# Finer pieces for the expert stages: mid-pass token turns, bf16 routing entries and a three-product down projection

## The chip, the cores and the metric

The kernel runs on one core of a Trainium2 chip. The metric is the device time of one execution in microseconds; less is better.

## The reference, cut to what matters

A two-layer backbone over 256 latent tokens and 256 context tokens of width 1024. Each layer has a token mixer (windowed attention in layer 0, a gated recurrence in layer 1) and then a mixture of experts. Layer 0's mixture runs on 512 tokens, layer 1's on 256.

```python
scores = sigmoid(t @ router_w)                      # 64 experts, 8 groups, top 8 of 4 groups
w = take(scores, idx) / sum * 2.5                   # gain of each (token, expert)
y = (silu(x @ w_gate[e]) * (x @ w_up[e])) @ w_down[e] * w   # x: the tokens routed to e
out = sum over the 8 experts of a token + shared expert
```

Each expert has three float32 matrices: gate and up of 1024 x 256, down of 256 x 1024, so 3 MiB in all.

## The kernel before

**Routing (`route_phase`).** For every token and expert the kernel writes an entry of three float32 numbers (`routes.entry`: token index less 8192, gain, destination row less 8192) and a slot number (`routes.slot`). The work is cut into blocks of S slots of one expert, S = 128 in layer 0 and 64 in layer 1. The phase also starts loading the first blocks' weights (`weights.prefetch`), once the normed rows are stored, and adds the shared expert's output.

**First expert stage (`expert_phase`, layer 0).** One block b after the other, 66 in this run. Two buffers q = b % 2 hold gate/up weights and down weights. Step b runs on five engines at once, each with its instruction order written out by hand and semaphores between them:

- TensorE (`step`, `down`, `turn_tokens`, `slots`): the gate and up products of block b in 4 chunks of 2 k-slices. Each float32 product is three float32r products (`x_hi*w_hi`, `x_lo*w_hi`, `x_hi*w_lo`), 24 matmuls of 512 columns (L1340). Then the 8 transposes of block b+1's tokens (L1313), the down projection of block b-1 in plain float32 (L1325; 4 matmuls, shown as 8 records), 2 transposes of block b's hidden rows (L1351), and the entry selection of block b+3 with a one-hot matrix (L1301; 4 matmuls, 8 records).
- ScalarE rounds block b+1's weights to float32r (`w_hi`, L1383, 4 chunks), writes `x_hi` (L1373), the SiLU (L1400), half of y (L1390) and the transposed hidden rows (L1407).
- VectorE subtracts to get `w_lo` (L1459, 4 chunks) and `x_lo` (L1451), multiplies the hidden rows with the gain (L1478), copies half of y (L1467), builds the one-hot matrix of block b+4 (`pick`, L1433, one instruction per token tile) and reads entries from PSUM (`indices`, L1442 and L1443). Its order in a step: w_lo chunks 0, 1, 2; hidden; w_lo chunk 3; x_lo; y; pick; indices.
- GpSimd only issues indirect DMAs: the scatter of block b-1's y rows (L1266) and the gather of block b+3's tokens (L1257).
- SP issues the weight loads (L899, L902), 1 MiB each. A gate/up load waits until the buffer's `w_lo` is made, a down load until the down projection that read the buffer is done (`y_done`).

**Second expert stage (`expert_pair_phase`, layer 1).** Two blocks of 64 slots side by side make a pair, 33 pairs in this run. All products are plain float32 (L1630, L1657). There is one buffer for gate, one for up and one for down; each is loaded again when the products that read it are done. SP's order: gates, ups, downs of pair i.

The code of the routing phase's entries and of both stages as they are before:

## Time and profile before

| | |
|---|---|
| median of 3 runs | 2326.23 us (2323.54 to 2328.62) |
| the profiled execution's own time | 2326.45 us |
| its span, first to last instruction | 2324.6 us |
| mean granted TensorE clock | 0.915 of full speed |
| TensorE busy | 1915.4 us (82%) |
| VectorE busy | 1145.3 us (49%) |
| ScalarE busy | 794.1 us (34%) |
| GpSimd busy | 318.6 us (14%) |
| HBM read and written | 596 MB and 56 MB |

PE is TensorE, PEld its weight loads, DVE VectorE, ACT ScalarE, POOL GpSimd; SP only issues DMAs. The end of a matmul is modelled and matmuls overlap, so for TensorE the distance from one start to the next is the time that counts. In a row of the timeline the first number is the start in us, the second the duration of the merged instructions, xN their count, and the bracket tells how long the engine idled before and what released it.

### The profile page before, as it was taken

What the parts mean: (1) busy time and instruction counts of PE and PEld (TensorE: products, weight loads), DVE (VectorE), ACT (ScalarE), POOL (GpSimd) and SP (SyncE); (2) the same over time, 40 slices, a digit from 0 to 9 for tenths busy, and PEclk for the clock granted to TensorE, in tenths of its full rate; (3) what the DMA queues carried; (4) which work ended last, traced back from release to release, by engine and by line L of the source; (5) the groups of instructions that cost most, each with busy time, mean ns of one, the idle gap of its engine ahead of it and who ended that gap; (6) DMA issues with size and microseconds to landing.
All of it is one profiled execution on the core that took longest, in us unless ns stands there. A gap on an engine that the chain in (4) does not pass through costs nothing. (4 is left out here: it accounts for less than half of the span.)

```text
span 2324.6 us, 33561 instructions
## 1 busy us (share of the span) xinstructions
PE 1915.4 (82%) x9971; PEld 1298.1 (56%) x9972; DVE 1145.3 (49%) x2242; ACT 794.1 (34%) x1292; POOL 318.6 (14%) x333
## 2 busy tenths in 40 slices
PE   2889897899999999999974987637778788878783
PEld 0778744467777777777741971103445555555551
DVE  2325622577777777777748565893131121212114
ACT  1214411155555555555521557870101111111110
POOL 0220010111111211211210101221001111111110
PEclk8999987899999999999987997768889999999997
DMA  6850055068998899999955416304439999999994
GB/s 239 296 188 1 1 224 202 9 251 323 339 339 330 327 342 345 348 333 343 330 191 220 137 55 194 109 18 128 185 144 418 414 392 388 400 411 402 418 366 173
DMA packets 139045, 597.07 MB, mean 257 GB/s; under 512 B 32632, under 2 KB 51128, under 8 KB 79728
## 3 DMA queue, kind: packets, MB, share of 16 engines
q1 hardware_dynamic: 103264, 509.97, 58.3%
q0 software_dynamic: 35584, 84.31, 9.7%
q10 hardware_dynamic: 144, 2.10, 0.2%
q8 instruction: 31, 0.51, 0.1%
q14 instruction: 22, 0.18, 0.0%
HBM read 596.17 MB, written 56.20 MB: 281 GB/s over the span
## 5 line engine op out<-in xcount | busy, mean ns | idle before, releaser
L1459 DVE TENSOR_TENSOR m_w_lo<-m_wgu,m_w_hi 128x1024 fp32r<-128x1024 f32 x264 | 312.6, 1221 | 170.6 <-ACT m_w_hi L1383 157.1
L1383 ACT ACTIVATE m_w_hi<-m_wgu 128x1024 fp32r<-128x1024 f32 x264 | 266.9, 1051 | 205.6 <-DMA m_wgu<-in_moe_w_up 153.0
L1630 PE MATMUL ps<-m_wgu,m_xT 128*64 128x256 f32 x2112 | 261.4, 403 | 78.9 <-DMA m_wgu<-in_moe_w_up 60.1
L1630 PEld LDWEIGHTS ps<-m_wgu,m_xT 128*64 128x64 f32 x2112 | 185.7, 145 | 165.8 <-issue 122.5
L1325 PE MATMUL ps<-m_wd,m_hidT 128*128 128x512 f32 x528 | 237.6, 593 | 0.3 <-ACT m_hidT L1407 0.3
L1340 PE MATMUL ps<-m_w_hi,m_x_hi 128*128 128x512 f32 x528 | 212.8, 403 | 7.2 <-DVE m_x_lo L1451 6.5
L1340 PE MATMUL ps<-m_w_lo,m_x_hi 128*128 128x512 f32 x528 | 208.1, 394 | 0.0
L1340 PE MATMUL ps<-m_w_hi,m_x_lo 128*128 128x512 f32 x528 | 207.2, 392 | 0.0
L1725 DVE SCALAR_TENSOR_TENSOR m_hid<-m_act_g,m_meta,ps 128x256 f32<-128x256 f32 x33 | 15.9, 480 | 337.9 <-ACT m_act_g L1679 337.9
L1325 PEld LDWEIGHTS ps<-m_wd,m_hidT 128*128 128x128 f32 x528 | 95.3, 190 | 95.1 <-issue 95.1
L1266 POOL DMA_INDIRECT y_rows<-h,m_sidx x66 | 67.5, 1023 | 554.5 <-DVE h L1467 554.5
L1657 PE MATMUL ps<-m_wd,m_hidT 128*64 128x512 f32 x528 | 122.3, 604 | 21.2 <-ACT m_hidT L1682 15.3
L1679 ACT ACTIVATE m_act_g<-ps 128x256 f32<-128x256 f32 x33 | 12.6, 383 | 315.7 <-PE ps L1630 315.7
L1340 PEld LDWEIGHTS ps<-m_w_hi,m_x_hi 128*128 128x128 f32 x528 | 100.2, 190 | 27.0 <-issue 7.5
L325 ACT ACTIVATE squares<-x_stream 128x1024 bf16<-128x1024 f32 x16 | 16.9, 1053 | 286.8 <-DVE x_stream L864 143.4
L1340 PEld LDWEIGHTS ps<-m_w_lo,m_x_hi 128*128 128x128 f32 x528 | 99.8, 189 | 21.4
L1340 PEld LDWEIGHTS ps<-m_w_hi,m_x_lo 128*128 128x128 f32 x528 | 100.3, 190 | 19.1
L1798 PE MATMUL ps<-c_rows,table 128*128 128x512 f32 x96 | 52.5, 709 | 51.0 <-DMA c_rows<-y_rows 51.0
L1575 POOL DMA_INDIRECT h<-h_rows,m_gidx x35 | 35.5, 1014 | 379.3 <-DVE m_gidx L1713 373.0
L1451 DVE TENSOR_TENSOR m_x_lo<-ps,m_x_hi 128x512 fp32r<-128x512 f32 x134 | 85.9, 682 | 0.5 <-ACT m_x_hi L1373 0.5
L1657 PEld LDWEIGHTS ps<-m_wd,m_hidT 128*64 128x64 f32 x528 | 42.1, 138 | 78.5 <-issue 78.5
L1433 DVE TENSOR_SCALAR m_onehot<-table,l_slot 128x128 f32<-128x128 f32 x280 | 78.2, 345 | 10.0 <-PE ps L1301 4.8
(316 smaller groups left out, 3429.9 us busy)
## 6 DMA issues: line engine op xcount, KB each, us to landing
m_wgu<-in_moe_w_gate SPq DMA_DIRECT2D x132, 1024.0 KB
m_wgu<-in_moe_w_up SPq DMA_DIRECT2D x132, 1024.0 KB
m_wd<-in_moe_w_down SPq DMA_DIRECT2D x132, 1024.0 KB, 9.9
c_rows<-y_rows SPq DMA_DIRECT2D x12, 2048.0 KB, 15.9
mods<-in_ada_w POOLq DMA_DIRECT2D x11, 1024.0 KB, 6.3
mods<-in_ada_w SPq DMA_DIRECT2D x11, 1024.0 KB, 4.8
mods<-in_lru_w_in SPq DMA_DIRECT2D x7, 1280.0 KB, 6.9
ada_w<-in_ada_w SPq DMA_DIRECT2D x8, 1024.0 KB, 17.5
```

Of the source, the lines that this page charges most:

```text
L325: act.activation(g.junk[:], g.x[:, t, :], ACT.Square, accum_out=g.sumsq[:, t:t + 1]).then_inc(self.squared, 1)
L1266: pool.indirect_dma_start(g.y_rows[0:tiles * P * TOPK, :], bass.IndirectOffsetOnAxis(ap=sidx[q][:, 0:1], axis=0), ysb[q], None, bounds_che ...
L1325: last = pe.matmul(g.ps[0:S, YB + n, :], hidT[:, j, :], wd[:, q, j, n * 512:(n + 1) * 512], start=(j == 0), stop=(j == KF - 1))
L1340: last = pe.matmul(g.ps[0:S, GU, :].rearrange("p (a f) -> p a f", a=2), x[:, q, k, :], w[:, :, k, :], start=(k == 0 and n == 0), stop=(k = ...
L1383: act.activation(w_hi[:, :, k, :], wgu[:, q, :, k, :], ACT.Copy).then_inc(hi_s, 1)
L1433: last = dve.tensor_scalar(onehot[:, q, t, :], g.field("iota")[:, 0:S], routes.slot[:, t, bass.ds(e, 1)], g.table[:, bass.ds(b + FIELD[f"n ...
L1451: dve.tensor_tensor(x_lo[:, q, ks, :], g.ps[:, XB + n, 0:4 * S].rearrange("p (k c) -> p k c", c=S), x_hi[:, q, ks, :].bitcast(F32), ALU.su ...
L1459: dve.tensor_tensor(w_lo[:, :, k, :], wgu[:, q, :, k, :], w_hi[:, :, k, :].bitcast(F32), ALU.subtract).then_inc(lo_s, 1)
L1575: pool.indirect_dma_start(xg, None, g.h2_rows[0:tiles * P, :], bass.IndirectOffsetOnAxis(ap=gidx[:, 0:1], axis=0), bounds_check=last_token ...
L1630: last = pe.matmul(g.ps[half[s], GU, a * FE:(a + 1) * FE], xT[:, k, half[s]], wgu[:, s, a, k, :], start=(k == 0), stop=(k == KD - 1))
L1657: last = pe.matmul(g.ps[half[s], YB + n, :], hidT[:, j, half[s]], wd[:, s, j, n * 512:(n + 1) * 512], start=(j == 0), stop=(j == KF - 1))
L1798: last = pe.matmul(g.ps[:, t % 2, :], g.ident, rows[:, 2 * (t % 2), k, :], start=(k == 0), stop=(k == TOPK - 1))
```

## The change

Five edits, in the order of the kernel:

1. Routing entries become bfloat16. Token index and destination are written as two or three exact pieces, the gain as three bfloat16 pieces found one after the other, so an entry has 9 numbers instead of 3. The constant pieces are written before the router's scores are awaited. The one-hot matrix is bfloat16 too and comes from a single `scalar_tensor_tensor` over all token tiles instead of a `tensor_scalar` for each. `indices` adds the three pieces with a `tensor_reduce` and then makes the index from its result.
2. First stage: the transposes of block b+1's tokens are moved from behind chunk 3 to behind chunk 1 (`TURN_AT = 1`), on ScalarE and VectorE as well.
3. First stage: the down projection becomes three float32r products (12 matmuls of 512 columns instead of 4 float32 ones). ScalarE makes `wd_hi` (2 copies of 128x1024 per block) and `hidT_hi`, GpSimd makes `wd_lo` (2 `tensor_tensor` of 128x1024 per block, `down_low`, ahead of the scatter and the gather in its order), VectorE makes `hidT_lo`. A down load now waits for `wd_lo` instead of `y_done`.
4. First stage: the down buffers and one gate/up buffer are placed in memory of `g.mods` that is free by then. This makes room and moves no data.
5. Second stage: gate and up weights have two buffers instead of one; the prefetch loads pair 1's gate and up as well, and the loops take two pairs a turn. In SP's order `gate_up(n, q)` loads the gates and ups of pair n+1 once the same products of pair n-1 are done.

```diff
-        self.entry = sb(n + "entry", [P, tiles, EXPERTS, 3])
+        self.entry = sb(n + "entry", [P, tiles, EXPERTS, 3 * PIECES], BF16)
...
-        self.wgu = sb(tag + "wgu", [P, 2, 2, KD, FE])
+        self.wgu = sb(tag + "wgu", [P, 2, 2, 2, KD, FE])
...
     def prefetch(self, sp):
...
+        for q in range(2):
+            for s in range(2):
+                self.gate(sp, 2 * q + s, q, s)
+            for s in range(2):
+                self.up(sp, 2 * q + s, q, s)
+            if q == 0:
+                for s in range(2):
+                    self.down(sp, s, s)
...
+                for t in range(tiles):
+                    chain.done(dve.memset(routes.entry[:, t, :, 0], t * P - FAR))
+                    chain.done(dve.memset(routes.entry[:, t, :, DEST * PIECES], TOPK * t * P - FAR))
+                chain.done(dve.memset(routes.entry[:, :, :, 2], 0.0))
+                chain.done(dve.tensor_copy(routes.entry[:, :, :, 1], tok0))
+                chain.done(dve.tensor_scalar(routes.entry[:, :, :, DEST * PIECES + 1], tok0, float(TOPK), None, ALU.mult))
                 dve.wait_ge(scored, 1)
...
-                chain.done(dve.tensor_tensor(routes.entry[:, :, :, 1], weight[:], wsum[:, :, None].to_broadcast([P, tiles, E]), ALU.mult))
-
+                chain.link(dve.tensor_tensor(weight[:], weight[:], wsum[:, :, None].to_broadcast([P, tiles, E]), ALU.mult))
+                for m in range(PIECES):
+                    piece = routes.entry[:, :, :, GAIN * PIECES + m]
+                    chain.link(dve.tensor_copy(piece, weight[:]))
+                    if m + 1 < PIECES:
+                        chain.link(dve.tensor_tensor(weight[:], weight[:], piece, ALU.subtract))
...
-                for t in range(tiles):
-                    chain.link(dve.tensor_scalar(wsum[:, t:t + 1], tok[:, t:t + 1], float(TOPK), -1.0 - FAR, ALU.mult, ALU.add))
-                    chain.done(dve.tensor_scalar(routes.entry[:, t, :, 2], kth[:, t, :], wsum[:, t:t + 1], None, ALU.add))
+                chain.done(dve.tensor_scalar(routes.entry[:, :, :, DEST * PIECES + 2], kth[:], -1.0, None, ALU.add))
...
-                    sp.wait_ge(y_done, b - 1)
+                    sp.wait_ge(wd_lo_s, KF * b - KF)
...
+                def down_low(i, q):
+                    b = 2 * i + q
+                    for j in range(KF):
+                        pool.wait_ge(wd_hi_s, KF * b + (j + 1))
+                        pool.tensor_tensor(wd_lo[:, q, j, :], wd[:, q, j, :], wd_hi[:, q, j, :].bitcast(F32), ALU.subtract).then_inc(wd_lo_s, 1)
+
...
                 with pool.Fori(1, final + 1) as i:
+                    down_low(i, 0)
                     scatter(i - 1, 1)
                     gather(i + 1, 1)
+                    down_low(i, 1)
                     scatter(i, 0)
                     gather(i + 2, 0)
...
-                    pe.wait_ge(hidT_s, b + 1)
-                    pe.wait_ge(wd_in[q], 16 * (i + 1))
+                    pe.wait_ge(hidT_split, b + 1)
+                    pe.wait_ge(wd_lo_s, KF * b + KF)
...
-                        for n in range(2):
-                            last = pe.matmul(g.ps[0:S, YB + n, :], hidT[:, j, :], wd[:, q, j, n * 512:(n + 1) * 512],
-                                             start=(j == 0), stop=(j == KF - 1))
+                        for m, (h, w) in enumerate(((hidT_hi, wd_hi), (hidT_hi, wd_lo), (hidT_lo, wd_hi))):
+                            for n in range(2):
+                                last = pe.matmul(g.ps[0:S, YB + n, :], h[:, j, :], w[:, q, j, n * 512:(n + 1) * 512],
+                                                 start=(j == 0 and m == 0), stop=(j == KF - 1 and m == 2))
...
-                    turn_tokens(i + q, 1 - q)
+                        if c == TURN_AT:
+                            turn_tokens(i + q, 1 - q)
...
                     if split:
-                        split_high(i + q, 1 - q, range(CHUNKS - 1))
+                        split_high(i + q, 1 - q, range(TURN_AT + 1))
+                    tokens(i + q, 1 - q)
+                    if split:
+                        split_high(i + q, 1 - q, range(TURN_AT + 1, CHUNKS - 1))
...
-                    tokens(i + q, 1 - q)
+                    down_high(i, q, range(1))
...
-                    act.activation(hidT[:], g.ps[:, HB, 0:KF * S].rearrange("p (j c) -> p j c", c=S), ACT.Copy).then_inc(hidT_s, 1)
+                    act.activation(hidT_hi[:], g.ps[:, HB, 0:KF * S].rearrange("p (j c) -> p j c", c=S), ACT.Copy).then_inc(hidT_s, 1)
+                    down_high(i, q, range(1, KF))
...
-                    for t in range(tiles):
-                        last = dve.tensor_scalar(onehot[:, q, t, :], g.field("iota")[:, 0:S], routes.slot[:, t, bass.ds(e, 1)],
-                                                 g.table[:, bass.ds(b + FIELD[f"negbase{layer}"][0], 1)], ALU.subtract, ALU.is_equal)
-                    last.then_inc(onehot_s, 1)
+                    dve.scalar_tensor_tensor(onehot[:, q, :, :], routes.slot[:, :, bass.ds(e, 1)].to_broadcast([P, tiles, S]),
+                                             g.table[:, bass.ds(b + FIELD[f"negbase{layer}"][0], 1)],
+                                             g.field("iota")[:, None, 0:S].to_broadcast([P, tiles, S]),
+                                             ALU.add, ALU.is_equal).then_inc(onehot_s, 1)
...
-                    dve.tensor_copy(meta[:, bass.ds(b, 1), :].rearrange("p o c -> p (o c)"), g.ps[0:S, MB + q, 0:3]).then_inc(meta_v, 1)
-                    dve.tensor_scalar(gidx[q][:], g.ps[0:S, MB + q, 0:1], FAR, None, ALU.add).then_inc(idx_s, 1)
+                    pieces = g.ps[0:S, MB + q, 0:3 * PIECES]
+                    dve.tensor_reduce(meta[:, bass.ds(b, 1), :].rearrange("p o c -> p (o c)"), pieces.rearrange("p (c m) -> p c m", m=PIECES),
+                                      AX.X, ALU.add).then_inc(meta_v, 1)
+                    dve.wait_ge(meta_v, b + 1)
+                    dve.tensor_scalar(gidx[q][:], meta[:, bass.ds(b, 1), 0], FAR, None, ALU.add).then_inc(idx_s, 1)
...
                     if split:
-                        split_low(i + q, 1 - q, range(CHUNKS - 1))
+                        split_low(i + q, 1 - q, range(TURN_AT + 1))
+                    tokens(i + q, 1 - q)
+                    if split:
+                        split_low(i + q, 1 - q, range(TURN_AT + 1, CHUNKS - 1))
...
-                    tokens(i + q, 1 - q)
...
+                    dve.wait_ge(hidT_s, b + 1)
+                    dve.tensor_tensor(hidT_lo[:], g.ps[:, HB, 0:KF * S].rearrange("p (j c) -> p j c", c=S), hidT_hi[:].bitcast(F32),
+                                      ALU.subtract).then_inc(hidT_split, 1)
                     pick(i + 2, q)
                     indices(i + 1 + q, 1 - q)
...
+                turns = rounds_after_first(sp)
+                with sp.Fori(0, turns) as m:
+                    gate_up(2 * m + 1, 0)
+                    down(2 * m + 1)
+                    gate_up(2 * m + 2, 1)
+                    down(2 * m + 2)
+                gate_up(2 * turns + 1, 0)
+                down(2 * turns + 1)
+                down(2 * turns + 2)
```

## Rows read from the trace of the kernel before

**Rows 1.** Busy us of each engine by stretch, then granted clock, DMA share, GB/s.

```profile
470.00:1190.00 720.00, 717.73 (x3275) 529.00 (x3275) 531.72 (x977) 397.80 (x587) 132.10 (x129) 1.00 0.88 325
809.04:819.96 10.92, 10.92 (x53) 8.04 (x52) 8.20 (x15) 6.14 (x10) 2.00 (x2) 1.00 0.89 322
1685.00:1722.00 37.00, 22.99 (x89) 14.26 (x89) 15.66 (x56) 1.75 (x4) 3.09 (x3) 0.72 0.06 18
1730.00:2260.00 530.00, 432.42 (x3094) 282.46 (x3091) 102.64 (x377) 61.36 (x125) 63.25 (x64) 0.96 1.00 404
```

**Rows 2.** TensorE in one block of the first expert stage, in order of time.

```profile
809.36 0.39 PE L1340 MATMUL ps<-m_w_hi,m_x_lo 128*128 128x512 f32 x1
...
814.61 1.04 PE L1313 MATMUL ps<-table,h 128*128 128x128 f32 x8
815.48 3.60 PE L1325 MATMUL ps<-m_wd,m_hidT 128*128 128x512 f32 x8
818.92 0.39 PE L1351 MATMUL ps<-table,m_hid 128*128 128x128 f32 x2
819.15 0.95 PE L1301 MATMUL ps<-l_entry,m_onehot 128*128 x8
```

**Rows 3.** Bf16 matmuls of the first routing phase, in order of time.

```profile
429.03 0.19 PE L1019 MATMUL ps<-r_chosen_bf,before_bf 128*128 128x64 bf16 x1
...
429.06 0.19 PE L1019 MATMUL ps<-r_chosen_bf,ones_bf 128*128 128x64 bf16 x1
```

**Rows 4.** The other engines around the same block, in order of time.

```profile
812.87 3.50 DVE L1459 TENSOR_TENSOR m_w_lo<-m_wgu,m_w_hi 128x1024 fp32r<-128x1024 f32 x3 [2.42 <-ACT m_w_hi L1383]
...
816.28 0.48 DVE L1478 SCALAR_TENSOR_TENSOR m_hid<-m_act_g,m_meta,ps 128x256 f32<-128x256 f32 x1
...
816.67 1.22 DVE L1459 TENSOR_TENSOR m_w_lo<-m_wgu,m_w_hi 128x1024 fp32r<-128x1024 f32 x1
...
817.81 1.28 DVE L1451 TENSOR_TENSOR m_x_lo<-ps,m_x_hi 128x512 fp32r<-128x512 f32 x2
...
819.12 0.69 DVE L1467 COPY h<-ps 128x512 f32<-128x512 f32 x1
...
820.04 1.12 DVE L1433 TENSOR_SCALAR m_onehot<-table,l_slot 128x128 f32<-128x128 f32 x4 [0.22 <-issue]
...
821.07 0.15 DVE L1442 COPY m_meta<-ps 128x3 f32 x1
...
822.21 1.01 POOL L1257 DMA_INDIRECT h<-h_rows,m_gidx  x1 [0.45 <-issue]
```

**Rows 5.** VectorE and GpSimd in the recurrence, in order of time.

```profile
1508.16 0.42 DVE L2212 TENSOR_TENSOR hsum<-hsum,h 80x256 f32<-80x256 f32 x1
...
1509.94 1.34 DVE L2211 TENSOR_TENSOR_SCAN h<-ls_a,h,ls_bu 80x256 f32<-80x256 f32 x1
...
1510.94 1.18 POOL L2159 TENSOR_TENSOR h<-ls_a 80x512 f32<-80x512 f32 x1 [0.20 <-ACT ls_a L2132]
1511.32 1.08 DVE L2212 TENSOR_TENSOR hsum<-hsum,h 80x256 f32<-80x256 f32 x1
```

**Rows 6.** GpSimd's tensor_tensor line in full: duration ns min/median/max.

```profile
L2159 POOL TENSOR_TENSOR h<-ls_a x32: 1030/1354/1482, 1417.0 to 1558.2; 80x512 f32<-80x512 f32 x32
```

**Rows 7.** VectorE and a GpSimd gather at the stage's start, in order of time.

```profile
461.54 4.63 DVE L1459 TENSOR_TENSOR m_w_lo<-m_wgu,m_w_hi 128x1024 fp32r<-128x1024 f32 x4
...
462.37 4.66 POOL L1257 DMA_INDIRECT h<-h_rows,m_gidx  x1 [4.41 <-PE ps L1313]
```

**Rows 8.** The scatters' time to landing, 600 to 700 us, then 1190 to 1199 us.

```profile
DMA to landing us min/median/max: 9.1/9.6/10.0
...
DMA to landing us min/median/max: 2.1/2.4/2.6
```

**Rows 9.** TensorE at the end of the second expert stage, in order of time.

```profile
2258.85 3.67 PE L1630 MATMUL ps<-m_wgu,m_xT 128*64 128x256 f32 x32 [0.39 <-DMA m_wgu<-in_moe_w_up]
...
2265.29 3.65 PE L1657 MATMUL ps<-m_wd,m_hidT 128*64 128x512 f32 x16 [0.56 <-ACT m_hidT L1682]
```

152 lines of the change are left out of this document (87 added, 65 removed).

## Prediction

> **What bounds the kernel now.** I read the windows by stage first. The two expert stages hold most of the time: blocks of layer 0 run from about 468 to 1196 us, pairs of layer 1 from about 1716 to 2269. In the first, TensorE is busy 717.73 of 720 us and the DMA engines only 0.88; in the second the DMA share is 1.00 and TensorE has gaps [rows 1]. So the first stage is set by TensorE, and one block of it, by TensorE's timeline, repeats every 10.92 us. The second is set by weight traffic. Then I took that block apart, start to start [rows 2]: 24 float32r matmuls 5.57 us (5.25 from the second one on, so 0.228 each), 8 token transposes 0.87, the float32 down projection 3.44, hidden transposes 0.23, entry selection 0.81. The sum is 10.92, with no hole.
>
> The other engines have room on paper: in the same 10.92 us VectorE is busy 8.20, ScalarE 6.14, GpSimd 2.00 [rows 1]. The question is what happens to VectorE and GpSimd once GpSimd computes.
>
> **TensorE's part.** Down goes from 3.44 us to 12 x 0.228 = 2.74. Entry selection goes from 8 records of float32 to 4 bf16 matmuls. Two bf16 matmuls of the routing phase start 0.03 apart [rows 3], and the present records are 0.10 apart, so it costs 0.12 to 0.40; I take 0.25. The transposes only move. TensorE alone could then do a block in 5.57 + 0.87 + 2.74 + 0.23 + 0.25 = 9.66 us, 1.26 less. Weight traffic is unchanged; at a share of 1.00 the block needs 0.89 x 10.92 = 9.7 us. Over 66 blocks that would be up to 80 us. I don't think it is reached.
>
> **VectorE's own work.** Start to start in its timeline [rows 4]: four w_lo chunks 4 x 1.14 (three take 3.50, one 1.22), hidden 0.39, x_lo with the small index 1.31. New or changed: y's copy gives way to hidT_lo after 0.61; hidT_lo to pick 0.92, which is what y to pick takes now (the wait for a register, 0.22 of it shown as issue, stays); pick as one instruction of 512 elements 0.61 like the copy of 512, against 1.12 now; the entries' sum and index 0.27, two dependent small ones of 0.15 or less. Sum: 4.56 + 0.39 + 1.31 + 0.61 + 0.92 + 0.61 + 0.27 = 8.67 us a block. That alone hides under 9.66.
>
> **GpSimd against VectorE.** In the recurrence both compute. A VectorE instruction reading two SBUF tensors that takes 0.42 us alone took 1.08 when it started 0.38 after a GpSimd tensor_tensor, and ended 0.28 after it; the GpSimd one ended 0.84 after the VectorE one before it had ended, and that one had been stretched too [rows 5]. So they exclude each other, and 512 elements hold GpSimd's turn for 0.84 us. All 32 of that line take 1.03 to 1.48 us, 1.35 in the middle, waits included [rows 6]. The new GpSimd instructions have 1024 elements, two a block. Their hold h lies between 2 x 0.84 = 1.68 and 2 x 1.35 = 2.7 us; I take 1.8, near the low end, since the high one has waits in it.
>
> On VectorE, w_lo (four) and the new pick read two SBUF tensors. The others read PSUM and don't collide. Now the order. The first half of wd_hi follows w_hi's chunk 3 on ScalarE, so GpSimd's first starts when w_lo chunk 3 ends. Pick would start 0.17 + 0.61 + 0.92 = 1.70 after that (0.17 for the scatter index), so it is late by h - 1.70. GpSimd's second has its half of wd_hi by then (hidT_hi and one copy after the hidden transposes, under 2 us by an estimate, against some 3) and starts when pick ends; only the sum and index (0.27) run beside it, so chunk 0 of the next block is late by h - 0.27. VectorE's round is 8.67 + 2h - 1.97 = 6.70 + 2h. I add 0.15 for each of two handovers (semaphore and start, an estimate from the 0.20 and 0.28 in rows 5): 7.0 + 2h. With h = 1.8 it is 10.6 us; with 1.68, 10.4. At h = 1.96 it equals 10.92. TensorE then waits about 0.9 us a block for the hidden rows, which now come later. The wait for wd_lo is not the late one. Counted from the start of w_lo chunk 3, TensorE's next step starts at about 0.7, and the second half is ready at 1.14 + 0.15 + 1.8 + 0.61 + 0.15 + 1.8 = 5.65, so 5.0 into the step; the down projection starts 5.57 + 0.87 = 6.4 into it. SP's down load waits for the same instruction; behind it in SP's queue is the gate/up load, which waits for a later w_lo anyway, so nothing is held.
>
> The Trainium skill (GPSIMD Engine Reference, 3.1 Elementwise) gives 4497 ns for a float32 tensor_tensor of 2048 elements, so an estimate of 2.25 us for 1024, against 1.9 from this trace; by the page the round would be 11.1 to 11.5 us and the change would lose, which is rival (b).
>
> ScalarE adds two wd_hi copies of the size of a w_hi chunk. Four of those are within its 6.14 us [rows 1], so the two cost at most 3.1: 9.2 of 10.6. They hide; without that cover they would cost up to 3.1 us a block. Moving the tokens takes x_lo off the end of VectorE's step, where its end at 819.09 leaves TensorE 0.9 us today [rows 2, 4].
>
> **The gather.** Today it is issued at 822.21 and its transposes begin two blocks on, at 814.61 + 2 x 10.92 = 836.45: 14.2 us. After, GpSimd does two subtractions and the scatter first, which puts the gather 6.5 us into the step, or 8.7 if the scatter has to let w_lo chunks 0 and 1 pass; I take 8. The transposes that need it begin 2.8 us into the next step: 5.4 us. A scatter lands 9.1 to 10.0 us after issue mid-stage and 2.1 to 2.6 on idle queues [rows 8]. Those 9 us are queueing: today the down load, the scatter, both gate/up loads and the gather are all issued within 3 us. In the new order they spread, and I take 5 us, just in time. Also, VectorE's back-to-back w_lo chunks can hold an indirect DMA: one took 4.66 us beside four of them, where 1.01 is usual [rows 7, 4]; that is where the 8.7 comes from.
>
> The Trainium skill (SBUF, Who interferes with whom) infers that a tensor_tensor doesn't hold back a DMA's descriptors; the row of 4.66 us speaks against it. By the page the gather would go out 1 to 2 us earlier, and the late gather below would be ruled out.
>
> **The rest.** Routing: VectorE gets a chain of five more copies and subtractions of 256 elements (one of that size takes 0.42 us [rows 5]), less nine smaller ones: +1 us in layer 0, +0.5 in layer 1; the memsets hide in the wait for the scores. The stages' starts: fewer one-hot instructions, shorter selection at a slow clock: -3 and -1.5. End of the first stage: the last block's down waits for wd_hi, GpSimd and hidT_lo: +2.5. Second stage: pair 1's gates and ups (4.2 MB, 10.4 us at 404 GB/s) load while the DMA share is 0.06 [rows 1]. But the tail grows: today TensorE needs 2265.29 + 3.65 - 2258.85 = 10.1 us after the last ups land [rows 9]; after, the last limiting load is the downs of the pair before, with one down (3.65), gates and ups (7.3) and the rest (6.4) behind it: 17.4. Net -3, between 0 and -10. Together about -3.5 us, between -12 and +3.
>
> **Sum.** 66 x (10.6 - 10.92) = -21; -21 - 3.5 = -24.5. Against the profiled execution's own 2326.45 us (span 2324.6, about 2 outside it), which is the median of the runs to 0.2: 2302 us.
>
> **The rivals.** (a) The exclusion is weaker than read, or the instructions fit in VectorE's pauses. Then TensorE and DMA bound the block at 9.9: -67 - 3.5, so 2256. For it: VectorE has 2.7 us free a block [rows 1]. Against: both stretched rows. Chance 0.18. (b) GpSimd is slow: h = 2.2, round 11.4: +32 - 3.5, so 2355. It decides from h = 1.96 on. For it: 1.35 in the middle of rows 6; against: 0.84 in rows 5. Chance 0.22, with ends from 2331 up. (c) The gather comes late. It counts over two blocks: period = (8 + landing + 6.85) / 2 (6.85 from the transposes to the step's end); 5 us gives 9.9, hidden; from 7.0 on it exceeds 10.92, 8 gives 11.4 and 2356. Chance 0.08, since a longer period also empties the queues. (d) No measurable change, h near 1.96 or the DMA engines at their real limit near 10.9 (the uneven rows of gathers and scatters may fill half of them): 2323. Chance 0.12. The forecast, round between 10.3 and 10.8, has 0.40; its own range is 2280 to 2318.
>
> **Numbers.** A measurement of this kernel tells 0.2%, 4.7 us. Faster: 0.40 + 0.18 = 0.58; same 0.12; slower 0.30. The range 2257 to 2352 leaves about 1 in 10 out on each side.
>
> **What would show it.** In the changed trace: a period of about 10.6 us; TensorE idle before the hidden transposes (released by m_hid) for 0.9 us; GpSimd's tensor_tensor at 1.9 to 2.1 us, more when waiting; w_lo's mean above 1.18 us, with chunk 0 stretched to some 2.5. If TensorE waits on the gather, (c); if w_lo isn't stretched, (a). DMA share near 0.92. In layer 1, 10 us earlier in the middle and 3 at the end. What would make it wrong is above all h, and how the two engines' turns fall.

## The result: 1.9% slower, and the profile after

The changed kernel takes 2370.97 us (median of 4, 2359.78 to 2379.16) beside 2325.78 for the kernel before in the same measurement: a ratio of 1.0193, 95% interval 1.0175 to 1.0211. The forecast was 2302, its range ended at 2352. The profiled execution has a span of 2369.4 us, 44.8 more than before. ScalarE's first and last SiLU of each expert stage, read from the timeline by their starts, cut the two spans into pieces:

| piece | before, us | after, us | difference |
|---|---|---|---|
| start to the first SiLU of stage 1 | 475.33 | 476.42 | +1.1 |
| 65 periods of stage 1 | 711.64 (10.95 each) | 759.27 (11.68 each) | +47.6 |
| last SiLU of stage 1 to the start of its last copy of y | 9.31 | 12.32 | +3.0 |
| from there to the first SiLU of stage 2 | 529.52 | 526.23 | -3.3 |
| 32 periods of stage 2 | 536.76 | 533.18 | -3.6 |
| the rest | 62.04 | 61.98 | -0.1 |

All the loss is in the period of the first stage. Everything else together is -2.8 us, where the prediction had -3.5.

Three rows of the page's groups for after (busy us, mean ns of one; then the idle time before them), which answer to GpSimd's new instruction and to [rows 7]:

```profile
L1290 POOL TENSOR_TENSOR m_wd_lo<-mods,m_wd_hi 128x1024 fp32r<-128x1024 f32 x132 | 369.2, 2811 | 182.3 <-ACT m_wd_hi L1421 182.0
...
L1504 DVE TENSOR_TENSOR m_w_lo<-mods,m_w_hi 128x1024 fp32r<-128x1024 f32 x132 | 231.6, 1775 | 22.0 <-ACT m_w_hi L1412 21.9
...
L1504 DVE TENSOR_TENSOR m_w_lo<-m_wgu,m_w_hi 128x1024 fp32r<-128x1024 f32 x132 | 169.7, 1294 | 42.8 <-ACT m_w_hi L1412 36.0
```

GpSimd's subtraction takes 2.81 us where 1.9 to 2.1 was foreseen, and w_lo, 1.2 us before, is stretched. TensorE was busy without a hole in [rows 1]; after, two windows, the middle of the stage and a stretch within one block:

```profile
core 0: us, PE busy (x) PEld busy (x) DVE busy (x) ACT busy (x) POOL busy (x), PEclk, DMA share, GB/s
...
500.00:1150.00 650.00, 593.38 (x2798) 478.32 (x2798) 570.26 (x726) 463.19 (x617) 470.67 (x224) 0.96 0.84 315
...
779.10:782.40 3.30, 3.27 (x9) 2.58 (x10) 3.27 (x7) 0.71 (x1) 3.15 (x2) 0.57 0.61 180
```

Neither TensorE (91%) nor VectorE (88%) is full. In the second window the mean granted clock is 0.57: it falls to half, the lower of its two levels (1.2 in place of 2.4 GHz), soon after the window's start. The timeline of that block, in order of time (start, duration, engine; in brackets the idle time before it; "issue" is idle time in which the profile shows nothing that the engine waits for):

```profile
773.65 0.38 ACT L1441 ACTIVATE m_act_g<-ps 128x256 f32<-128x256 f32 x1 [0.31 <-PE ps L1368]
...
774.94 1.22 DVE L1504 TENSOR_TENSOR m_w_lo<-mods,m_w_hi 128x1024 fp32r<-128x1024 f32 x1
776.02 2.35 POOL L1290 TENSOR_TENSOR m_wd_lo<-mods,m_wd_hi 128x1024 fp32r<-128x1024 f32 x1 [2.45 <-ACT m_wd_hi L1421]
776.07 0.47 DVE L1526 SCALAR_TENSOR_TENSOR m_hid<-m_act_g,m_meta,ps 128x256 f32<-128x256 f32 x1
776.46 2.99 DVE L1504 TENSOR_TENSOR m_w_lo<-mods,m_w_hi 128x1024 fp32r<-128x1024 f32 x1
776.69 0.47 PE L1380 MATMUL ps<-table,m_hid 128*128 128x128 f32 x2 [0.32 <-DVE m_hid L1526]
777.85 0.55 PE L1328 MATMUL ps<-l_entry,m_onehot 128*128 x4 [0.68 <-issue]
778.61 3.09 POOL L1290 TENSOR_TENSOR m_wd_lo<-mods,m_wd_hi 128x1024 fp32r<-128x1024 f32 x1 [0.24 <-ACT m_wd_hi L1421]
779.13 0.47 PE L1368 MATMUL ps<-m_w_hi,m_x_hi 128*128 128x512 f32 x1 [0.73 <-issue]
...
780.17 0.63 PE L1368 MATMUL ps<-m_w_hi,m_x_hi 128*128 128x512 f32 x1
780.37 1.88 DVE L1474 SCALAR_TENSOR_TENSOR m_onehot<-l_slot,table 128x512 bf16<-128x512 f32 x1
780.60 0.63 PE L1368 MATMUL ps<-m_w_hi,m_x_lo 128*128 128x512 f32 x1
```

Two things are to be read here. First the exclusion: GpSimd's subtraction, started first, takes 2.35 and ends at 778.37; w_lo beside it ends 1.08 later, about its own length; GpSimd's next one ends 2.25 after that w_lo, and pick 0.55 after that. Second TensorE: the SiLU was done at 774.03, but the hidden rows come at 776.07, behind w_lo chunk 2 in VectorE's order. After the wait for them follow 0.68 and 0.73 us of "issue", and then some eight matmuls 0.43 apart where 0.228 was the pace, so about 1.6 us lost. The visible wait of 0.32 us before the hidden transposes is rare: 4 of the 63 steps below have one of over 0.15 us, where the prediction expected 0.9 us a block. The idle time stands behind the transposes, 0.33 us a block before the selection and 0.48 behind it, and 19 of the 63 steps have a run of matmuls at half clock.

TensorE's steps, start to start, mean of the first 63 complete ones of each trace (a wait is in the part before it), in us. The four kernels on the right are experiments below:

| | before | after | no_low | half_low | fp32_late | late_swap |
|---|---|---|---|---|---|---|
| gate and up | 5.58 | 6.33 | 6.14 | 6.39 | 5.68 | 5.56 |
| token transposes | 0.88 | 0.84 | 0.86 | 0.83 | 0.89 | 0.89 |
| down | 3.44 | 2.87 | 2.77 | 3.01 | 3.44 | 3.44 |
| hidden transposes | 0.23 | 0.70 | 0.23 | 0.67 | 0.34 | 0.23 |
| entry selection | 0.85 | 0.99 | 0.88 | 0.98 | 0.53 | 0.10 |
| step | 10.97 | 11.73 | 10.88 | 11.89 | 10.88 | 10.22 |

The down projection did become 0.6 shorter. The part of the hidden transposes is 0.5 longer, which is mostly the idle time before the selection; the selection gives nothing back; and gate and up, whose work is the same, take 0.75 more: 0.52 of it is pace (matmuls over 0.35 apart are 10% of them, 0.4% before), 0.15 a late gather. A rival can be dropped here: TensorE doesn't wait for `wd_lo` or `hidT_lo`, since none of its waits of over 0.15 us in these steps stands in front of the down projection.

In the second stage the loads of gate and up no longer hold TensorE; the downs do, for more time in total than all three loads before (88 us against 83), and the period falls by 0.7% all the same (the waits in that stage, us in total, times, longest):

```profile
PE ps L1727 <- DMA m_wd<-in_moe_w_down: 88.1, 29, 5.3
```

### The profile page after: what moved, and what is told of

The parts are those of the page before. It is cut to its first block and busy times, and to the rows that moved or that the text cites. A ratio compares the mean times of both kernels' runs of the same rounds, so it can differ in the third digit from the quotient of the medians.

```text
span 2369.4 us, 33304 instructions
## 1 busy us (share of the span) xinstructions
PE 1883.7 (79%) x9819; PEld 1307.4 (55%) x9820; DVE 1270.6 (54%) x2007; ACT 937.5 (40%) x1424; POOL 733.6 (31%) x465
## 5 line engine op out<-in xcount | busy, mean ns | idle before, releaser
L1290 POOL TENSOR_TENSOR m_wd_lo<-mods,m_wd_hi 128x1024 fp32r<-128x1024 f32 x132 | 369.2, 2811 | 182.3 <-ACT m_wd_hi L1421 182.0
L1504 DVE TENSOR_TENSOR m_w_lo<-mods,m_w_hi 128x1024 fp32r<-128x1024 f32 x132 | 231.6, 1775 | 22.0 <-ACT m_w_hi L1412 21.9
L1699 PE MATMUL ps<-m_wgu,m_xT 128*64 128x256 f32 x2112 | 236.6, 382 | 1.2 <-DVE m_xT L1793 1.2
L1727 PE MATMUL ps<-m_wd,m_hidT 128*64 128x512 f32 x528 | 161.4, 767 | 94.6 <-DMA m_wd<-in_moe_w_down 93.3
L1504 DVE TENSOR_TENSOR m_w_lo<-m_wgu,m_w_hi 128x1024 fp32r<-128x1024 f32 x132 | 169.7, 1294 | 42.8 <-ACT m_w_hi L1412 36.0
L1412 ACT ACTIVATE m_w_hi<-m_wgu 128x1024 fp32r<-128x1024 f32 x132 | 139.8, 1059 | 113.2 <-PE ps L1368 113.2
L1412 ACT ACTIVATE m_w_hi<-mods 128x1024 fp32r<-128x1024 f32 x132 | 139.5, 1059 | 55.3 <-PE ps L1368 43.4
L1421 ACT ACTIVATE m_wd_hi<-mods 128x1024 fp32r<-128x1024 f32 x132 | 139.2, 1055 | 0.0
L1808 DVE COPY h<-ps 128x512 f32<-128x512 f32 x33 | 22.8, 691 | 170.7 <-PE ps L1727 170.7
L1283 POOL DMA_INDIRECT y_rows<-h,m_sidx x66 | 105.6, 1600 | 14.0 <-issue 8.1
```

The costliest lines, as they stand in the source:

```text
L1283: pool.indirect_dma_start(g.y_rows[0:tiles * P * TOPK, :], bass.IndirectOffsetOnAxis(ap=sidx[q][:, 0:1], axis=0), ysb[q], None, bounds_che ...
L1290: pool.tensor_tensor(wd_lo[:, q, j, :], wd[:, q, j, :], wd_hi[:, q, j, :].bitcast(F32), ALU.subtract).then_inc(wd_lo_s, 1)
L1412: act.activation(w_hi[:, :, k, :], wgu[q][:, :, k, :], ACT.Copy).then_inc(hi_s, 1)
L1421: act.activation(wd_hi[:, q, j, :], wd[:, q, j, :], ACT.Copy).then_inc(wd_hi_s, 1)
L1504: dve.tensor_tensor(w_lo[:, :, k, :], wgu[q][:, :, k, :], w_hi[:, :, k, :].bitcast(F32), ALU.subtract).then_inc(lo_s, 1)
L1699: last = pe.matmul(g.ps[half[s], GU, a * FE:(a + 1) * FE], xT[:, k, half[s]], wgu[:, q, s, a, k, :], start=(k == 0), stop=(k == KD - 1))
```

## The experiments

All edits are to the changed kernel unless said. "Period" is the mean distance of the SiLUs in stage 1, in us; ratios are to the kernel before. A period comes from the one profiled execution of each kernel, which can lie off the median of all its runs: half_low's is 14 us above it (0.2 us a block), slots_hid's 9 and fp32_late's 8. no_low, half_low, half_hid, half_slots and nolow_turn2_slots leave out all or half of the low part of the down weights, so their output is incomplete.

**bench: the disputed price by itself.** GpSimd's and VectorE's instructions on tiles of the stage's sizes, between the layers, four of each.

```python
pool.tensor_tensor(wd_lo[:, q, j, :], wd[:, q, j, :], wd_hi[:, q, j, :].bitcast(F32), ALU.subtract)
dve.tensor_tensor(w_lo[:, :, k, :], wgu[:, :, k, :], w_hi[:, :, k, :].bitcast(F32), ALU.subtract)
```

> The changed kernel with seven short parts between the two layers, for their durations alone, each of four instructions an engine on tiles of the sizes of the first expert stage. GpSimd's subtraction of 128x1024 alone; VectorE's alone; both at once; GpSimd's beside VectorE subtractions of 1024 that read PSUM and SBUF; beside ScalarE's copies; a GpSimd copy of 1024 beside VectorE's subtractions; GpSimd's subtraction beside VectorE instructions with one SBUF input. Theory: GpSimd alone takes 2.25 to 2.4 us, so h was put 0.5 us too low (1.8 in the forecast); both at once take turns, about 4 x 2.3 + 4 x 1.14 = 13.8 us in all; no stretch beside PSUM reads, beside ScalarE or beside one-input instructions. Rival: alone it takes 1.8 to 1.9 us and the 2.8 us in the stage is waiting; or both run side by side at reduced speed, under 11 us in all.

The timeline of bench (both at once; beside PSUM reads; beside ScalarE; a GpSimd copy beside w_lo):

```profile
1348.51 9.23 POOL L1868 TENSOR_TENSOR b_wd_lo<-b_wd,b_wd_hi 128x1024 fp32r<-128x1024 f32 x4 [95.73 <-PEq L1853]
...
1362.77 11.06 DVE L1882 TENSOR_TENSOR b_w_lo<-b_wgu,b_w_hi 128x1024 fp32r<-128x1024 f32 x4
...
1362.93 13.09 POOL L1868 TENSOR_TENSOR b_wd_lo<-b_wd,b_wd_hi 128x1024 fp32r<-128x1024 f32 x4 [5.20 <-DVE b_w_lo L1882]
...
1376.06 2.48 DVE L1877 TENSOR_TENSOR b_w_lo<-ps,b_w_hi 128x512 fp32r<-128x512 f32 x4 [2.23 <-POOL b_wd_lo L1868]
...
1385.61 3.90 ACT L1890 ACTIVATE b_w_hi<-b_wgu 128x1024 fp32r<-128x1024 f32 x4 [37.49 <-POOL b_wd_lo L1868]
...
1394.74 6.97 POOL L1866 CAST b_wd_lo<-b_wd_hi 128x1024 fp32r<-128x1024 f32 x4
```

And two of its lines by themselves (durations min/median/max in ns):

```profile
L1868 POOL TENSOR_TENSOR b_wd_lo<-b_wd,b_wd_hi x20: 2328/2348/3317, 1348.5 to 1411.2; 128x1024 fp32r<-128x1024 f32 x20
...
L1880 DVE TENSOR_SCALAR b_w_lo<-b_w_hi x4: 693/2824/2829, 1402.9 to 1409.0; 128x1024 fp32r<-128x1024 f32 x4
```

Alone GpSimd needs 9.23 / 4 = 2.31 us; both at once need 13.1 for four and four, close to the sum 9.23 + 4 x 1.14. PSUM reads (0.62 each for 512 elements) and ScalarE's copies (0.98) aren't touched. So h is 2.3. One expectation failed: a `tensor_scalar` of 1024 elements whose only input is in SBUF is held as well, 0.69 us free, 2.82 beside GpSimd. It isn't the number of SBUF inputs alone: the instruction that read PSUM has one SBUF input too, and wasn't held. The Trainium skill (GPSIMD Engine Reference, 3.1 Elementwise) gives 4497 ns for 2048 elements, so an estimate of 2.25 us for 1024; bench agrees with its 2.31.

**no_low, half_low: none and one of GpSimd's two subtractions.**

```diff
-                        for m, (h, w) in enumerate(((hidT_hi, wd_hi), (hidT_hi, wd_lo), (hidT_lo, wd_hi))):
+                        for m, (h, w) in enumerate(((hidT_hi, wd_hi), (hidT_hi, wd_hi), (hidT_lo, wd_hi))):   # no_low
-                    down_low(i, 0)
-                    down_low(i, 1)
```

The waits of TensorE and SP for `wd_lo` become waits for `wd_hi`. half_low keeps the second half's subtraction and its waits.

> The changed kernel without GpSimd's subtractions: the third product of each half reads wd_hi once more in place of wd_lo, so the low part of the down weights is left out, with the same twelve matmuls, the same copies on ScalarE and everything else in place. Theory (the two engines exclude each other, and GpSimd's two turns a block, about 2.3 us each, are what VectorE's round of 7.0 + 2h = 11.6 us is made of): without them VectorE has 8.7 us of work and TensorE bounds the block at 9.9 to 10.2 us, so 65 x (10.05 - 11.68) = -106 us against the changed kernel's 2371, about 2265. Rival (TensorE's own path: the hidden rows stand behind w_lo chunk 2 in VectorE's order, the entry selection waits for a register behind them, and the clock falls after the idle time, with GpSimd or without): idle 1.08 and slow clock 0.62 us a block stay in good part, 11.2 us or more, 2340 or more. If the DMA engines are at their limit near 10.4 us a block: about 2288, TensorE waiting for the gather.

> The changed kernel with one of GpSimd's two subtractions a block: the first half's third product reads wd_hi in place of wd_lo (that half's low part is left out), the second half's subtraction stays. Theory (each turn of 2.3 us that GpSimd takes from VectorE costs about the same): half way between no_low's 10.85 and the changed kernel's 11.68, about 11.25 us a block, 2332 to 2345. Rival (only the first turn, which meets w_lo chunk 3 and pick, delays the hidden rows, or only the pile of two does): as no_low, 2304 to 2316, in which case the second turn is free; or as the changed kernel, above 2360.

no_low: 2309.07 us, 0.9911 (0.9895 to 0.9928), period 10.85. half_low: 2375.92, 1.0200 (1.0177 to 1.0222), period 11.85, as slow as with both. no_low met none of its three expectations (2265, 2288, 2340 or more); half_low met its rival. So GpSimd's work costs 0.83 us a block, more than the whole loss of 0.73, but not as a sum of turns, and without it the block is far from 9.9: in no_low's table column 0.88 for the selection (0.48 of it idle) and, within gate and up, 0.33 of waits for the gather. half_low's window and one of its blocks:

```profile
500.00:1150.00 650.00, 598.81 (x2747) 482.95 (x2746) 515.76 (x713) 456.77 (x605) 278.36 (x164) 0.93 0.84 311
```

```profile
650.65 2.99 DVE L1474 SCALAR_TENSOR_TENSOR m_onehot<-l_slot,table 128x512 bf16<-128x512 f32 x1 [0.54 <-issue]
650.68 2.40 POOL L1290 TENSOR_TENSOR m_wd_lo<-mods,m_wd_hi 128x1024 fp32r<-128x1024 f32 x1 [7.67 <-ACT m_wd_hi L1421]
...
656.07 0.39 ACT L1441 ACTIVATE m_act_g<-ps 128x256 f32<-128x256 f32 x1 [0.30 <-issue]
...
658.47 0.47 DVE L1526 SCALAR_TENSOR_TENSOR m_hid<-m_act_g,m_meta,ps 128x256 f32<-128x256 f32 x1
...
659.09 0.47 PE L1380 MATMUL ps<-table,m_hid 128*128 128x128 f32 x2 [0.30 <-DVE m_hid L1526]
660.23 0.55 PE L1328 MATMUL ps<-l_entry,m_onehot 128*128 x4 [0.66 <-issue]
661.50 0.47 PE L1368 MATMUL ps<-m_w_hi,m_x_hi 128*128 128x512 f32 x1 [0.73 <-issue]
```

VectorE is busy for 79% only. One collision (pick, 0.75 free, takes 2.99) delays the three w_lo chunks and x_lo behind it, the hidden rows come 2.0 us after the SiLU, TensorE then has 0.30 + 0.66 + 0.73 idle, and the next block runs some eight of its matmuls at half clock, 0.43 us apart, from the fifth on (11.7 us for the step, where no_low's quick ones take 10.2). The expectations' "some 14 matmuls" is too many; their 1.6 us is right. In that block VectorE catches up, and the collision falls on pick again: 31 of the 63 steps have the wait, and 30 the slow matmuls.

**slots_first, hid_first, slots_hid, half_hid, half_slots: what a late hidden row costs.** Two moves, alone and together: the selection ahead of the wait on TensorE, the hidden rows ahead of w_lo chunk 2 on VectorE.

```diff
+                    slots(i + 1 + q, 1 - q)          # slots
                     pe.wait_ge(hid_s, b + 1)
...
                     last.then_inc(hid_turned, 1)
-                    slots(i + 1 + q, 1 - q)          # slots
...
                     tokens(i + q, 1 - q)
-                    if split:                        # hid
-                        split_low(i + q, 1 - q, range(TURN_AT + 1, CHUNKS - 1))
...
-                        split_low(i + q, 1 - q, range(CHUNKS - 1, CHUNKS))
+                        split_low(i + q, 1 - q, range(TURN_AT + 1, CHUNKS))
```

> The changed kernel with one step moved on TensorE: the entry selection of the next block is issued ahead of the wait for the hidden rows in place of behind the hidden transposes. It fills the idle time before the transposes (0.33 us a block on average) and takes the register load off the path (0.33 and part of 0.48). Theory (VectorE's round with GpSimd's turns sets the period): TensorE waits just as long elsewhere, the period stays within 0.2 us of 11.68, 2358 to 2375. Rival (TensorE's own waits and the clock that falls after them are the loss): 0.6 to 0.8 us of idle gone and 0.3 to 0.6 of slow clock with it, 10.4 to 10.8 us a block, 2290 to 2315.

> The changed kernel with one order changed on VectorE: the hidden rows ahead of w_lo chunk 2 in place of behind it. All work, GpSimd's subtractions included, stays, and the output is complete. Theory (a late hidden row costs not only its own time: TensorE's queue then has a register load and a branch in the open, and the clock falls to half for some 14 matmuls, 1.6 us, in the block after): the hidden rows come 1.1 us earlier, the waits before the hidden transposes go, most of the half clock (0.62 us a block) goes with them, 10.9 to 11.2 us a block in place of 11.68, 2320 to 2340. Rival (VectorE's round with GpSimd's turns is the bound at 7.0 + 2h = 11.6): the order is without effect, 2360 to 2375.

> slots_first with the hidden rows ahead of w_lo chunk 2 on VectorE. The output is complete. Theory: slots_first has 0.19 us of waiting before the hidden transposes and 0.26 before or behind the selection left, and 0.62 for the gather; the first part goes, the gather's lateness stays, 11.0 to 11.2 us a block, 2328 to 2342. If the gather's lateness is only where another wait would be, 11.3 as before, 2345 to 2352.

> half_low (one subtraction a block on GpSimd, the first half's low part left out) with the hidden rows ahead of w_lo chunk 2 on VectorE. Theory (in half_low the hidden rows are 1.1 us late in every other block, and behind that come the register load, the branch and 1.6 us of half clock; VectorE itself has 2 us to spare): the waits before the hidden transposes go and the half clock with them, 10.8 to 11.1 us a block in place of 11.85, 2308 to 2330. Rival (something else holds half_low, the subtraction that the down projection waits for or VectorE after all): 11.6 or more, 2355 or more.

> half_low with the entry selection ahead of the wait for the hidden rows on TensorE. Theory: the selection and its register load run in the time in which the hidden rows are late, so the idle stretches are shorter and the clock stays up: 10.7 to 11.0 us a block, 2300 to 2322. Rival: as half_low, 2360 or more.

| | us | ratio (interval) | period | VectorE busy, 500 to 1150 us | wait for the gather, per block | extra pace of gate/up, per block |
|---|---|---|---|---|---|---|
| after | 2370.97 | 1.0193 | 11.68 | 88% | 0.15 | 0.62 |
| slots_first | 2347.20 | 1.0093 (1.0073 to 1.0113) | 11.29 | 98% | 0.62 | 0.21 |
| hid_first | 2375.11 | 1.0211 (1.0186 to 1.0237) | 11.67 | 97% | 0.33 | 0.34 |
| slots_hid | 2396.73 | 1.0300 (1.0275 to 1.0325) | 12.19 | 92% | 1.24 | 0.62 |
| half_low | 2375.92 | 1.0200 | 11.85 | 79% | 0 | 0.87 |
| half_hid | 2343.94 | 1.0076 (1.0049 to 1.0103) | 11.29 | 87% | 0.66 | 0.33 |
| half_slots | 2351.57 | 1.0107 (1.0078 to 1.0135) | 11.35 | 88% | 0.98 | 0.38 |

```profile
500.00:1150.00 650.00, 586.42 (x2881) 459.74 (x2880) 636.24 (x751) 486.48 (x635) 480.01 (x232) 1.00 0.85 325
```

That is slots_first's window; VectorE's 636.24 us is 98%. slots_first landed between its theory and its rival. hid_first didn't gain anything: the half clock went down as foreseen, but VectorE was then full. Its rival had 11.6 for the round 7.0 + 2h, and with bench's 2.31 it is 11.62. Where VectorE has time to spare, in half_hid, the same move brings 32 us (ratio of medians 0.987) and most of the idle time and half clock go, but half of what they free comes back as waits for the gather, up to 5.6 us at a time, and the 10.8 to 11.1 us expected weren't reached. half_slots missed its 10.7 to 11.0 in the same way. slots_hid missed altogether: it waits for the gather

```profile
PE ps L1340 <- DMA h<-h_rows,m_gidx: 71.5, 37, 3.8
```

in two thirds of its blocks (500 to 1170 us). It isn't the transfer: from issue to landing a gather takes 8.7 us in the middle, 8.6 in slots_first. It is issued later, on average 7.7 us after the start of TensorE's step, 6.4 in slots_first. Why the two subtractions and the scatter in front of it finish later there stays open.

**slots_turn2, nolow_turn2_slots: more time for the gather.** slots_first, with and without the subtractions, with the tokens one chunk later.

```diff
-        TURN_AT = 1
+        TURN_AT = 2
```

> slots_first with the tokens one chunk later (behind the third chunk in place of the second), so the gather has 1.4 us more. The three products and GpSimd's subtractions stay. The output is complete. Theory (in slots_first the gather's lateness, 0.62 us a block, is part of the loss and comes from GpSimd doing subtractions first): the waits for the gather fall below 0.2 us a block, the period from 11.29 to 10.8 to 11.0, 2318 to 2330, near the kernel before. Rival (VectorE's round with GpSimd's turns is the bound at 11.3 and the gather's waits only stand where other waits would): 11.2 to 11.4, 2342 to 2352.

> no_low (no subtractions on GpSimd, the low part of the down weights left out) with the entry selection ahead of the wait for the hidden rows and the tokens one chunk later, so slots_turn2 without GpSimd's subtractions. Theory (without GpSimd's turns the rest of no_low's 10.85 us is the register load and branch around the selection, 0.48, the late gather, 0.34, and the clock, 0.24): 9.9 to 10.2 us a block, 2250 to 2268, so against slots_turn2 GpSimd's turns cost 1.0 us a block. Rival (the DMA engines hold any kernel of this traffic at 10.8): 2303 to 2310.

slots_turn2: 2334.07 us, 1.0038 (1.0025 to 1.0052), period 11.07; nolow_turn2_slots: 2268.31, 0.9748 (0.9733 to 0.9763), period 10.16. slots_turn2 just missed its theory: the waits for the gather fell from 0.62 only to 0.39 us a block, and 2334 lies above the 2330. nolow_turn2_slots is at the edge of its own, with 0.38 of such waits. Between the two lies GpSimd alone: 0.9 us a block, as between after and no_low. The 10.16 also shows that neither the rest of the structure nor the DMA engines (358 GB/s there) force 10.8.

**fp32_down, fp32_pool, fp32_late, fp32_late_slots: the change without its down projection.** The down projection in float32 as before; with GpSimd's work kept but unused; with the tokens back behind chunk 3; with the selection moved.

```diff
-                        for m, (h, w) in enumerate(((hidT_hi, wd_hi), (hidT_hi, wd_lo), (hidT_lo, wd_hi))):
...
+                            last = pe.matmul(g.ps[0:S, YB + n, :], hidT[:, j, :], wd[:, q, j, n * 512:(n + 1) * 512],
+                                             start=(j == 0), stop=(j == KF - 1))
...
-                        if c == TURN_AT:             # fp32_late
-                            turn_tokens(i + q, 1 - q)
+                    turn_tokens(i + q, 1 - q)
```

> The changed kernel with the down projection of the first expert stage in plain float32 again: no wd_hi, no wd_lo, no hidT_lo, no subtraction on GpSimd; bf16 entries, tokens in the middle of the pass and the second stage's double buffers stay. The output is complete. Theory: TensorE bounds the block at 10.5 to 10.7 us (10.95 before, less the shorter entry selection), 65 x (10.6 - 10.95) = -23 us against before, -3 from the second stage, about 2300. Rival (mid-pass tokens put hid behind w_lo chunk 2 on VectorE, and TensorE idles before the hidden transposes whatever GpSimd does): 0.5 us or more of idle a block and a slower clock behind it, 11.1 us or more, 2330 or more.

> fp32_down with the two wd_hi copies on ScalarE and the two subtractions on GpSimd put back, their results unused, so that TensorE's work is that of fp32_down and nothing of it waits for them. The output is complete. Theory (GpSimd's two turns of 2.3 us come out of VectorE's time whether or not TensorE needs the result): the round is 8.39 + 4.6 less what falls beside PSUM reads and pauses, some 11.5 us against 11.07, so fp32_down's 2336 plus 25 to 45, 2361 to 2381. Rival (the cost of GpSimd's work in the changed kernel was the wait for wd_lo or for hidT_lo, not the exclusion): within 8 us of fp32_down, 2330 to 2344.

> The float32 down projection again as in fp32_down, and the tokens back at the end of the pass, as the kernel before has them; of the change only the bf16 entries (with one-instruction picks) and the second stage's double buffers stay. The output is complete. Theory (fp32_down lost 0.32 us a block to a gather that the earlier tokens made late, and some 0.1 to the broken pass): the tokens are needed 2.8 us later, the waits for the gather go, the block takes 10.97 - 0.33 (shorter entry selection) = 10.6 to 10.7 us, 65 x (-0.3) - 3 (second stage) - 2 (starts) = -25, about 2302. Rival (the bf16 selection gives nothing back, because TensorE's queue then waits for the register load and the branch in any order): 10.9 to 11.0 us, about 2320 to 2325.

> fp32_late, and on TensorE the entry selection ahead of the wait for the hidden rows, as in slots_first. The output is complete. If the idle time around the entry selection is the queue's (a register load and a branch behind a wait), the move hides most of what fp32_late has left of it, 0.1 to 0.4 us a block, 10.3 to 10.5 us, 2285 to 2298. If TensorE is held by the hidden rows instead, it is the same as fp32_late within 3 us.

fp32_down: 2336.54 us, 1.0033 (1.0017 to 1.0049), period 11.07: the time that its rival gave (2330 or more), but not by the rival's way. No step waits before the hidden transposes; 0.32 us a block go to waits for the gather and 0.29 to "issue" before gate and up. Mid-pass tokens cost more than the shorter selection gives. fp32_pool: 2344.57, 1.0069 (1.0050 to 1.0088), period 11.38: its 8 us over fp32_down lie at the edge of the rival, while the profiled executions are 0.31 us a block apart, 20 us in the stage. In either reading GpSimd's turns cost less here than the 0.8 to 0.9 us a block of the three-product kernels; that a longer step of TensorE hides them is the likely reason, not shown. fp32_late: 2310.26, 0.9925 (0.9910 to 0.9940), period 10.86, 8 us short of its theory; fp32_late_slots: 2312.83, 0.9937 (0.9923 to 0.9951), the same, so moving the selection didn't bring the 12 to 25 us of its first expectation. In fp32_late many steps take 10.2 us and then one waits. What it waits for:

```profile
644.10 0.34 SPq L903 DMA_DIRECT2D mods<-in_moe_w_gate  x1
644.53 1.28 SPq L903 DMA_DIRECT2D mods<-in_moe_w_up  x1
...
650.76 1.28 DVE L1485 TENSOR_TENSOR m_x_lo<-ps,m_x_hi 128x512 fp32r<-128x512 f32 x2
...
652.68 0.33 SPq L906 DMA_DIRECT2D mods<-in_moe_w_down  x1
653.99 0.33 SPq L903 DMA_DIRECT2D m_wgu<-in_moe_w_gate  x1
...
657.90 2.95 ACT L1405 ACTIVATE m_w_hi<-mods 128x1024 fp32r<-128x1024 f32 x3 [4.46 <-DMA mods<-in_moe_w_up]
```

w_lo of the block was made when x_lo started, at 650.76, so the next gate/up load could have gone out then; it went out 3.2 us later, behind the down load that waits for y. ScalarE waits 4.46 us for an up load.

**late_swap, late_swap_slots, before_swap, after_swap: the order of the loads.** fp32_late with SP's order changed, then with the selection moved; and the same order in the kernels before and after.

```diff
                 gate_up(1, 1)
-                down(1, 0)
                 with sp.Fori(2, final + 1) as i:
                     gate_up(i, 0)
-                    down(i - 1, 1)
+                    down(i - 1, 0)
                     gate_up(i, 1)
-                    down(i, 0)
+                    down(i - 1, 1)
+                down(final, 0)
                 down(final, 1)
```

> fp32_late with one order changed on SP: each gate/up load is issued ahead of the down load that stood in front of it (that down load waits for y of an earlier block, and the gate/up load stood behind it for up to 11 us of waiting). The output is complete. Theory (fp32_late's waits come from gate/up loads that are issued late, its blocks without a wait take 10.2 us): the waits of ScalarE for the up loads go, the block takes 10.2 to 10.4 us in place of 10.86, 65 x (-0.55) = -36, about 2275. Rival (the DMA engines are at their limit at a share of 0.9, whatever the order): 10.8 us, 2304 to 2314.

> late_swap, and the entry selection ahead of the wait for the hidden rows. The output is complete. If waits for loads are gone in late_swap, the move hides what the queue needs around the selection, 0 to 0.1 us a block: late_swap less 0 to 7 us. If the DMA engines are the limit, as fp32_late_slots, 2308 to 2315.

> The kernel before with SP's order of late_swap alone (each gate/up load ahead of the down load that stood in front of it). The output is complete. Theory (TensorE is busy 99.7 percent there and doesn't wait for loads): no change, 2321 to 2330; the gain of late_swap comes from both edits together, the shorter selection (which alone gave 16 us) and the order that then lets it count. Rival (the loads already cost the kernel before something that its TensorE row hides): 2310 or less.

> The changed kernel with SP's order of late_swap alone. The output is complete. Theory (its loads of gate and up aren't late: ScalarE waits for none of them, since the down load waits for GpSimd's subtraction in place of y, a step earlier): no gain, 2362 to 2376. If the order also brings the gather earlier (9.9 us of waits): down to 2355.

late_swap: 2277.26 us, 0.9788 (0.9774 to 0.9803), as expected. Its window, and a block of TensorE:

```profile
500.00:1130.00 630.00, 630.00 (x2838) 452.26 (x2837) 508.79 (x740) 393.37 (x556) 126.15 (x124) 1.00 0.93 357
```

```profile
800.84 1.05 PE L1335 MATMUL ps<-table,h 128*128 128x128 f32 x8
801.73 3.60 PE L1347 MATMUL ps<-mods,m_hidT 128*128 128x512 f32 x8
805.16 0.39 PE L1373 MATMUL ps<-table,m_hid 128*128 128x128 f32 x2
805.39 0.25 PE L1323 MATMUL ps<-l_entry,m_onehot 128*128 x4
...
811.07 1.05 PE L1335 MATMUL ps<-table,h 128*128 128x128 f32 x8
```

TensorE is full at full clock with a step of 10.2 us; the selection takes 0.10. late_swap_slots is the same (2277.61, 0.9782, 0.9765 to 0.9798): with no waits there is nothing for the move to hide. before_swap is 0.9992 (0.9983 to 1.0002), no change: the new order alone brings nothing, fp32_late's part of the change alone 17 us, both together 49 (some 4 of them in the second stage). after_swap missed: 2399.43, 1.0328 (1.0295 to 1.0361). There the down weights are needed a step earlier, by ScalarE's rounding, and now they are late (ScalarE waits for them; it has no such wait in the changed kernel):

```profile
ACT m_wd_hi L1421 <- DMA mods<-in_moe_w_down: 77.1, 46, 4.2
```

late_swap has complete output and is the fastest complete version found, 94 us faster than the changed kernel.

## Why the prediction was wrong

- **What bounds the kernel now:** right. TensorE was full; before_swap, with other loads in time, changes nothing.
- **The hold h, "I take 1.8, near the low end":** this is the first of two steps that failed. It measures 2.31 to 2.35 (bench). The prediction's own round 7.0 + 2h then gives 11.6 to 11.7, and its sum 66 x (11.62 - 10.92) - 3.5 = +43 us; measured were +44.8. Rival (b) had this mechanism with h = 2.2, and 2355. The low row of 0.84 for 512 elements was itself cut out of two overlapping durations; twice its middle value, 1.35, would have been 0.4 too high.
- **That the period is VectorE's round, with TensorE's 9.66 us as the only other floor:** this is the second step that failed. With h at nothing, no_low still takes 10.85 us a block, more than the 10.6 forecast with h = 1.8, so the right h alone would not have made the sum sound, and part of the agreement above is luck. In after VectorE isn't full. slots_first has the same order on VectorE and gets round in 11.29 at 98%, so 7.0 + 2h is at least 0.33 too long with the measured h, and 0.39 of after's 11.68 isn't VectorE's. half_low shows the limit that the sum didn't have: hidden rows 2.0 us behind the SiLU in every second block (0.5 in no_low), 1.4 us of issue in the open behind them, 1.6 us of half clock in the next block. The prediction had TensorE waiting 0.9 us a block for hidden rows, and took that wait as slack without a price; after has almost no such wait (4 of 63 steps), but pays in issue and clock.
- **TensorE alone 9.66 us, and rival (a):** the work terms were right or generous (2.77 for down against 2.74, 0.10 for the selection against 0.25). But no_low, where the exclusion is gone, needs 10.85, not 9.9. With slots_turn2's two moves the idle time around the selection goes and the waits for the gather stay (0.38), and the block takes 10.16.
- **The gather "just in time":** right at a price of 0.15 us a block in after, but by two errors that cancel: it is issued 5.8 us into TensorE's step in place of 8, and it lands 8.1 us later in the middle in place of 5. It had little to spare, and it is late in most of the variants with the tokens in mid-pass (0.3 to 1.0 us a block in the quicker ones, 1.24 in slots_hid). Moving the tokens ahead by two chunks is what brought it there: fp32_down to fp32_late, which moves them back, is worth 26 us. GpSimd's indirect DMAs do take longer beside VectorE, as the prediction read from its row of 4.66 us: of the 126 in the changed kernel's first expert stage, the 86 that run beside w_lo or pick take 1.58 us on average, the other 40 take 1.01. The gathers' landing times, from 500 to 1150 us:

```profile
DMA to landing us min/median/max: 5.2/8.1/11.2
```

- **The rest:** -2.8 against -3.5; the tail +3.0 against +2.5, the second stage -3.6 against -3.
- **DMA engines at their limit near 10.9, in rival (d):** no; late_swap moves 357 GB/s at a share of 0.93.

Open: whether the 0.68 us before the selection is the register load and the 0.73 behind it the loop's branch. Both stand there in the code, in every second block the second is 0.3, and slots_first removes the first; a kernel that loads the register earlier wasn't tried. Open too is why the clock falls in some blocks and not in others with the same waits: 0.73 us idle before a step doesn't lower it in no_low, and 19 of after's 63 steps are slow. That the slow matmuls follow late hidden rows is seen in half_low and goes with the moves in half_hid and half_slots; no run changes the clock alone.

## What to carry to other kernels

GpSimd arithmetic on SBUF and VectorE instructions with two SBUF inputs take turns at full length (13.1 us for four and four in bench); measure the hold alone before using it in a sum. What that costs the kernel is another question: two holds, one and none gave 11.68, 11.85 and 10.85 us a block. A wait on a full TensorE costs more than its length: in half_low a wait of 0.30 us in every second block comes with 1.4 us of issue and 1.6 us lost to the clock. When a shorter step brings nothing, look for the next thing in line in a queue: here one down load that stood in front of a gate/up load held back two thirds of the gain.

## What the runs showed of the hardware

- GpSimd's subtraction of 128x1024: 2.31 us alone; beside VectorE's, the two take turns (13.1 us for four and four). A VectorE `tensor_scalar` whose one input is in SBUF is held too (0.69 to 2.82 us); a `tensor_tensor` of one PSUM and one SBUF input (0.62 us for 512 elements) and ScalarE's copies (0.98) aren't.
- Four bf16 matmuls of 9 columns cost TensorE 0.10 us start to start in late_swap; from the first of the same four to the next step's first matmul it is 0.88 to 0.99 in no_low and after, 0.48 of it idle.
- After idle stretches of 0.32, 0.68 and 0.73 us around the selection the granted clock was 0.57 over 3.3 us (779.1 to 782.4 us of after); matmuls were 0.43 apart in place of 0.228. In no_low stretches of 0.73 us alone left it at full speed.
